# Moving the weighted sums, the low parts of the weights and the modulation stream in a one-core three-block forward pass

## Chip, cores and metric

One Trainium2 chip, one of its cores. The metric is the device time of one execution in microseconds; before the change it is 2541.97 us, the median of three runs (2541.0 to 2543.16).

## The reference, cut to what matters

Two blocks work on 512 tokens of width 2048. The first has an attention layer and a pooling layer, the second is a layer of stick-breaking attention and retention. Each layer computes `shift, scale, gate = silu(c) @ mod_w + mod_b`, normalises, multiplies with a large input matrix, mixes, gates with `silu(z)`, and multiplies with an output matrix. For this change the attention layer matters:

```python
s = jnp.einsum('bqkgd,bskd->bkgqs', q, k).astype(jnp.float32) * ATTN_SCALE
p = jax.nn.softmax(s, axis=-1).astype(v.dtype)
o = jnp.einsum('bkgqs,bskd->bqkgd', p, v)          # the weighted sum
y = jnp.concatenate([outA, outB], axis=-1) * jax.nn.silu(z)
```

There are 16 heads of 128. Heads 0 to 7 see all 512 tokens and 256 context rows; heads 8 to 15 see a band of up to 384 tokens, the 256 context rows and a sink. All of it is float32.

## The kernel before, in words

**Weights.** All weight matrices are one stream of 376 chunks of 128x1024 floats. SyncE loads chunk i into `RAW[i % 5]`. A float32 product is made from rounded parts: ScalarE copies the chunk to fp32r (`WHI[i % 4]`, the plan's stage "split"), VectorE subtracts (`WLO`, in the place of `RAW`, stage "low"), and TensorE adds hi*hi, hi*lo and lo*hi. ScalarE may round chunk i once TensorE has finished chunk i - 4; VectorE's subtraction waits for ScalarE's rounding of the same chunk.

**The plan.** `make_plan` writes one list of stages, and each engine's program walks the whole list and issues what it has for each stage. So the list fixes the order on every engine, and each engine is held up only by its semaphore waits. A matrix product of 128 tokens by 256 columns goes through `gemm`: 4 chunks, each of 4 steps ("mm" of 6 matmuls). After each step `step(background)` advances the background generators by one: this is how attention is put between matrix products. `split_ahead(i)` is called once per chunk, in its second step, ahead of that step's background work. It first puts "low" for every chunk that has a "split" but no "low", then "split" for chunk i + 3. So in the attention heads VectorE makes the low part of a chunk one chunk later in the list than ScalarE rounds it: where ScalarE rounds chunk i + 3, VectorE makes the low part of chunk i + 2.

**A pair of heads.** For p = 0 to 7 there are two products (q, then z), 32 steps, and `pair_task(p)` runs beside them and beside the next pair's q product. Its clock t counts steps from the first score row. There are eight score rows (two heads of four 128-query tiles, n = 0 to 7), put at t = 0, 3, 6, 9, 17, 20, 23, 26 (in the last pair the last four one step sooner). For a row TensorE makes the scores in PSUM (`ST`, two halves by turns), VectorE takes the maximum (L1925) and bounds it (L1684), ScalarE takes the exponential (L1498, or L1493 and L1495), and one step later in the list ("row_end") VectorE takes the reciprocal (L1947), scales (L1684) and transposes (L1952). After a head's last row SyncE writes the probabilities out ("turn", 4 steps later) and reads them back in another layout ("turn_in", 8 steps later). The weighted sum ("pv") of the head is put 20 (first head of the pair) or 19 steps after its last row, at t = 29 and t = 45, and "gate" (VectorE, Y<-ST,Y) one step behind it. A new pair starts every 32 steps, so t = 29 is 3 steps ahead of the next pair's row 0 and t = 45 is the next pair's t = 13. The weighted sum writes the PSUM bank `OB`, which is part of the half that rows with odd n use, so it waits for the exponential of the last odd row. The last head, 15, is moved by DMAs that SyncE and ScalarE issue (L1116) once the sum of head 14 has been made.

**Modulation.** `mod_stream` is a generator: each step loads 512 KB (SyncE, L1176) and adds 2 x 512 columns on VectorE (`MACC`, L1687). It is stepped once per chunk, and a second time in chunks whose number is in `at["extra"]`. In the heads it is stepped once per chunk.

**Layer changes.** `gemm_last`, then `gemm_three`: the last product of a layer, the norm, and the first products of the next layer. There too the low parts follow `split_ahead`.

Of the kernel before, what the change touches and what calls it, by code (L numbers as in the profile page):

```python
# [79 lines left out]
def build(nc, ctx, T, out):  # L80
# [26 lines left out]
    for i in range(NR):  # L107
        tile, at = place(f"RAW{i}", [P, 4, 256], F32)
# [4 lines left out]
    for i in range(2):  # L113
        tile, at = place(f"MRAW{i}", [P, 4, 256], F32)
# [233 lines left out]
    def make_plan():  # L348
# [1 line left out]
        todo = []  # L350
        background = []
        gates = [[], [], []]
        at = {"load": 0, "split": 0, "low": 0, "use": 0, "done": 0, "unit": 0, "pair": 0, "heads": False, "hold": False, "extra": ()}
        scored = []
        summed = set()
        pending = []
# [2 lines left out]
        def put(*stage):  # L359
            todo.append(stage)  # L360
# [14 lines left out]
            put("split", at["split"])  # L375
            at["split"] += 1

        def low_next():
            put("low", at["low"])
            at["low"] += 1  # L380

        def split_ahead(i):
            while at["low"] < at["split"]:
                low_next()
            while at["split"] < min(i + NS, len(chunks)):
                split_next()

        def low_until(i):
            while at["low"] <= i:
                low_next()  # L390

        def step(gens):
            for g in list(gens):
# [13 lines left out]
        def unit(work, quiet=False):  # L407
            u = at["unit"]
            at["unit"] += 1
            n = len(units[u])  # L410
            at["pair"] += n // 8 + 1
            for c in range(n):
                i = at["use"]
                at["use"] += 1
                while at["split"] <= i:
                    split_next()
                low_until(i)
                work(u, i, c, c == n - 1)
                used(i)
                if not at["heads"]:  # L420
                    reduce_pending()
                if not (quiet and c >= n - 2 or at["hold"]):
                    step([mods])
                    if c in at["extra"]:
                        step([mods])
            return u
# [15 lines left out]
        def gemm_three(layer, tiles):  # L442
            first = at["pair"] % 2
            for pair in range(3):
                gated(pair)
            pairs = (first, 1 - first, 2)
            u, i0 = at["unit"], at["use"]
            at["unit"] += 1
            at["pair"] += 2
            at["use"] += 12  # L450
            next(tiles)
            split_ahead(i0 - 1)
            low_until(at["split"] - 1)
            next(tiles)
            for jj in range(2):
                for uu in range(3):
                    low_until(i0 + uu)
                    for nt in range(2):
                        put("mm2", "h", layer, u, i0 + uu, uu, 0, nt, jj, pairs[uu])
                    if jj:  # L460
                        used(i0 + uu)
                    if (jj, uu) != (1, 0):
                        split_ahead(i0 + (uu if jj else 0))
                        low_until(at["split"] - 1)
                    if (jj, uu) in ((0, 1), (1, 1)):
                        next(tiles)
            for c in range(3, 12):
                i, uu = i0 + c, c % 3
                low_until(i)
                for jj in range(2):  # L470
                    for nt in range(2):
                        put("mm2", "h", layer, u, i, uu, c // 3 * 4, nt, jj, pairs[uu])
                    if jj == 0:
                        split_ahead(i)
                        low_until(at["split"] - 1)
                        next(tiles, None)
                used(i)
                if layer == 2 and c >= 8:
                    reduce_pending()
                    step([mods])  # L480
            return u, first

        def gemm_last(layer):
            pair = at["pair"] % 2
            gated(pair)
            u, i0 = at["unit"], at["use"]
            at["unit"] += 1
            at["pair"] += 1
            at["use"] += 4
            spare[layer] = 1 - pair, i0 + 4  # L490
            s = 0
            for nt in range(2):
                for c in range(4):
                    low_until(i0 + c)
                    for jj in range(2):
                        put("mm", "y", layer, u, i0 + c, c, nt, jj, pair, c == 3)
                        if jj == 0:
                            if nt == 0:
                                split_ahead(i0)
                            elif c in (1, 2):  # L500
                                split_ahead(i0 + c)
                        step(background)
                        if s == 7:
                            put("o_copy", layer, 14, pair, 0, u, (u, 0))
                        elif s == 8:
                            put("o_more", layer, 14)
                        elif s in (11, 13, 14):
                            put("o_sum", layer, (11, 13, 14).index(s))
                        s += 1
                    if nt:  # L510
                        used(i0 + c)
                    elif c % 2:
                        reduce_pending()
                        step([mods])
            return u, pair
# [93 lines left out]
        def prologue():  # L609
            for i in range(8):  # L610
                put("job_load", i)
            for n in range(6):
                for q in range(4):
                    put("x_turn", n, q)
                put("x_sum", n)
            put("x_rstd")
            ready, near = [], []
            for i, (nb, c) in enumerate(jobs0):
                n = i // 4
                put("job_row", i)  # L620
                if i + 8 < len(jobs0):
                    put("job_load", i + 8)
                if i in (1, 3, 5):
                    load_next()
                if c == 3:
                    put("row_copy", n)
                if i == 3:
                    put("x_cast")
                if i in (9, 11, 13):
                    split_next()  # L630
                    low_next()
                    loads()
                if c == 1 and n > 0:
                    put("row_cols", n - 1)
                    ready += near
                    near = []
                    if n % 2 == 0:
                        put("h_pair", n // 2 - 1)
                        near = pieces(n // 2 - 1)
                if i > 51 and i % 4 == 3:  # L640
                    put("x_spill", i // 4 - 13, i)
                for _ in range((0, 2, 0, 3)[i % 4]):
                    if ready:
                        kv_piece(*ready.pop(0))
            put("row_cols", len(order0) - 1)
            put("h_pair", 7)
            put("x_spill", 3, 63)
            for piece in ready + near + pieces(7):
                kv_piece(*piece)
            at["unit"], at["use"], at["pair"] = 1, 8, 2  # L650
# [8 lines left out]
        def kv_piece(k, what, part):  # L659
            put("kv", k, what, part)  # L660
            if k % 4 == 3 and part == (1 if what == "k" else 2):
                used(at["done"])
                split_next()
                low_next()

        prologue()

# [19 lines left out]
        for i in range(3):  # L687
            put("v_copy", 0, i, 1, 0)
        task = chain([norm_rope(("k", 0), True), norm_rope(("kc", 0), True),
                      norm_rope(("k", 1), True), norm_rope(("kc", 1), True)])  # L690
        background.append(task)
        u, pair = gemm("hc", 1)
        finish(task)
        for nt in range(2):
# [1 line left out]
        task = chain([norm_rope(("k", 2), False), norm_rope(("k", 3), False)])  # L696
        background.append(task)
        pair = at["pair"] % 2
        at["extra"] = (0, 1, 2, 3)
        u = gemm_tok(1, 6, pair)  # L700
        at["extra"] = ()
        for i in range(3):
# [18 lines left out]
        def pair_task(p):  # L721
# [15 lines left out]
            def later(t, *stage):  # L737
                events.setdefault(t, []).append(stage)
# [7 lines left out]
            t, last_y = 0, 12  # L746
            while events:
                for what, *a in reversed(events.pop(t, [])):
                    if what == "rows":
                        i, qt = divmod(a[0], 4)  # L750
                        h, n = 2 * p + i, 8 * p + a[0]
# [4 lines left out]
                        if qt == 3:  # L756
                            later(t + 4, "turn", h)
                            if h < 15:
                                later(t + 8, "turn_in", h)
                            later(t + (10 if h == 15 else 20 - i), "pv", h)  # L760
                    elif what == "pv":
                        put("pv", *a)
                        later(t + 1, "gate", *a)
# [23 lines left out]
        for p in range(8):  # L787
            u, pair = gemm("h", 1)
# [887 lines left out]
    def dve_program(e):  # L1676
# [48 lines left out]
        for stage, *a in plan:  # L1725
# [43 lines left out]
            elif stage == "h_pair":  # L1769
                i, = a  # L1770
# [20 lines left out]
                for k in (2 * i, 2 * i + 1):  # L1791
                    e.wait_ge(a_h, ("c", k))
                    stt(CLO[:, k, :], TM[:, k % 2 * CTX:k % 2 * CTX + CTX], MODX[:, k:k + 1], f(CHI[:, k, :]), ADD,
                        SUB).then_inc(*v_h.up(("c", k)))
            elif stage == "low":
                i, = a
                e.wait_ge(a_whi, i)
                tt(WLO[i % NR][:, :, :], RAW[i % NR][:, :, :], f(WHI[i % NS][:, :, :]), SUB).then_inc(*v_wlo.up(i))
# [903 lines left out]
```

## Time and profile before

| | us |
|---|---|
| median of three runs | 2541.97 |
| the profiled execution | 2541.1 |
| its span, first to last instruction | 2539.1 |
| TensorE busy | 2463.3 (97%) |
| VectorE busy | 1713.5 (67%) |
| ScalarE busy | 932.6 (37%) |

The profile is of one execution. Its own time is 2.0 us over its span and 0.9 us under the median. Times in a timeline count from the first instruction. The attention heads lie between 258.7 us (the first maximum) and 787.9 us (the last).

### The profile page before, as it was taken

The page shows a single profiled execution, that of the slowest core. Times are in us where ns is not written, and L with a number is a line of the kernel's source. Part 1 is how long each engine was busy: PE and PEld are TensorE (multiplying, and loading weights), DVE is VectorE, ACT ScalarE, POOL GpSimd, SP SyncE. Part 2 cuts the span into 40 slices and gives each one's busy share as a digit, 9 for nine tenths or more (in the row PEclk, how much of TensorE's full clock was granted, in tenths as well). Part 3 has the DMA queues.
Part 4 walks back from the last instruction along what each step waited for, and adds up shares of the span by engine and source line. Part 5 has one row for each costly group of instructions (what it writes and reads, how often), then busy time and mean ns, then how long its engine had stood idle before and what let it go on. Part 6 is the DMA issues. An engine that isn't in the chain of part 4 may idle for free.

```text
span 2539.1 us, 29369 instructions
## 1 busy us (share of the span) xinstructions
PE 2463.3 (97%) x11527; PEld 1983.2 (78%) x11527; DVE 1713.5 (67%) x2634; ACT 932.6 (37%) x1453; POOL 111.5 (4%) x117
## 2 busy tenths in 40 slices
PE   7999999999889999999999999999999999999999
PEld 4789777777667887888888887888888787887887
DVE  4456888888877778776877767456455577666622
ACT  4232333333334333432334433445355432333421
POOL 0000000000000114000000113000000000000000
PEclk8999999999999999999999999999999999999999
DMA  9955678777766764666655754422222245532342
GB/s 348 337 187 189 203 206 223 214 220 207 203 180 188 256 197 151 204 203 215 203 166 170 253 182 136 125 83 84 83 84 83 81 144 166 178 120 83 126 156 83
DMA packets 345660, 439.32 MB, mean 173 GB/s; under 512 B 13154, under 2 KB 271842, under 8 KB 339762
## 3 DMA queue, kind: packets, MB, share of 16 engines
q1 hardware_dynamic: 338048, 403.82, 51.5%
q0 software_dynamic: 5808, 32.84, 3.4%
q8 instruction: 91, 1.49, 0.2%
q10 hardware_dynamic: 1666, 0.79, 0.1%
q14 instruction: 47, 0.39, 0.1%
HBM read 395.44 MB, written 40.37 MB: 172 GB/s over the span
## 4 chain that ended last, share of the span: by engine, by line
PE 79%; DVE 13%; ACT 2%; DMA 2%; issue 2%; SPq 1%; ACTq 0%; POOL 0%; DVEq 0%; POOLq 0%
PE G L2227 67%; PE ST L2227 12%; DVE SM L1925 2%; DVE MACC L1687 2%; DVE WLO L1681 1%; DVE PB L1952 1%; DVE PB L1684 1%; ACT PB L1498 1%; DMA MORE<-in_ev_mod_w 1%; DMA MRAW<-in_ev_mod_w 1%; DVE Y L1681 1%; DVE TT L1681 1%; PE ST L2230 0%; DVE SM L1684 0%; SPq L1162 0%
## 5 line engine op out<-in xcount | busy, mean ns | idle before, releaser
L2227 PE MATMUL G<-HHI,WHI 128*128 128x512 f32 x2596 | 1044.4, 404 | 2.9 <-DVE HLO L1681 2.4
L2227 PE MATMUL G<-HLO,WHI 128*128 128x512 f32 x2560 | 998.8, 390 | 2.4 <-DVE HLO L1687 2.4
L2227 PE MATMUL G<-HHI,WLO 128*128 128x512 f32 x2560 | 999.0, 390 | 0.0
L1325 ACT ACTIVATE WHI<-RAW 128x1024 fp32r<-128x1024 f32 x376 | 396.5, 1055 | 608.5 <-PE G L2227 547.0
L2227 PEld LDWEIGHTS G<-HHI,WHI 128*128 128x128 f32 x2596 | 488.8, 188 | 110.8 <-issue 7.7
L2227 PEld LDWEIGHTS G<-HLO,WHI 128*128 128x128 f32 x2560 | 481.4, 188 | 108.7 <-issue 7.7
L2227 PEld LDWEIGHTS G<-HHI,WLO 128*128 128x128 f32 x2560 | 480.6, 188 | 103.4
L1681 DVE TENSOR_TENSOR WLO<-RAW,WHI 128x1024 fp32r<-128x1024 f32 x376 | 460.7, 1228 | 93.8 <-ACT WHI L1325 93.5
L1687 DVE SCALAR_TENSOR_TENSOR MACC<-MWIDE,SC,MACC 128x512 f32<-128x512 f32 x420 | 320.8, 764 | 98.6 <-DMA MWIDE<-in_w_ada 48.1
L2227 PE MATMUL G<-WHI,HHI 128*128 128x512 f32 (+1 forms) x384 | 143.2, 373 | 0.6 <-ACT K L1325 0.6
L2227 PE MATMUL G<-WLO,HHI 128*128 128x512 f32 (+1 forms) x384 | 136.4, 355 | 0.0
L2227 PE MATMUL G<-WHI,HLO 128*128 128x512 f32 (+1 forms) x384 | 136.1, 354 | 0.0
L2227 PE MATMUL ST<-PT,VV 128*128 128x512 f32 (+2 forms) x192 | 93.7, 647 | 37.2 <-ACT PB L1498 34.5
L2227 PEld LDWEIGHTS ST<-PT,VV 128*128 128x128 f32 x192 | 42.2, 227 | 85.4 <-issue 77.6
L1322 ACT ACTIVATE SQ<-SQ 128x512 f32<-128x512 f32 x144 | 90.5, 628 | 28.4 <-DVE SQ L1687 25.2
L2227 PEld LDWEIGHTS G<-WHI,HHI 128*128 128x128 f32 x384 | 72.6, 189 | 18.3 <-issue 7.0
L2227 PEld LDWEIGHTS G<-WHI,HLO 128*128 128x128 f32 x384 | 72.7, 189 | 12.2 <-issue 1.7
L1498 ACT ACTIVATE PB<-ST,SM,COL 128x768 f32<-128x768 f32 x32 | 31.8, 994 | 135.0 <-DVE SM L1684 132.6
L2227 PEld LDWEIGHTS G<-WLO,HHI 128*128 128x128 f32 x384 | 72.7, 189 | 10.3
L1684 DVE TENSOR_SCALAR TM<-ST 128x512 f32<-128x512 f32 (+1 forms) x28 | 18.8, 672 | 78.8 <-ACT TY L1322 78.8
L1952 DVE STREAM_TRANSPOSE PB<-PB 128x768 f32<-128x768 f32 (+1 forms) x64 | 59.4, 928 | 2.2
L1925 DVE TENSOR_REDUCE SM<-ST 128x1 f32<-128x768 f32 (+2 forms) x64 | 54.6, 853 | 6.0 <-PE ST L2227 5.0
(273 smaller groups left out, 2431.2 us busy)
## 6 DMA issues: line engine op xcount, KB each, us to landing
RAW<-in_w_in SPq DMA_DIRECT2D x128, 512.0 KB, 3.7
MWIDE<-in_od_mod_w SPq DMA_DIRECT2D x96, 512.0 KB, 4.7
MWIDE<-in_w_ada SPq DMA_DIRECT2D x96, 512.0 KB, 4.7
RAW<-in_ev_w_in SPq DMA_DIRECT2D x80, 512.0 KB, 6.7
RAW<-in_od_w_in SPq DMA_DIRECT2D x64, 512.0 KB, 3.9
p_spill<-PB SPq DMA_DIRECT2D x15, 1536.0 KB, 6.3
PT<-p_spill SPq DMA_DIRECT2D x60, 384.0 KB, 7.6
MWIDE<-in_ev_mod_w SPq DMA_DIRECT2D x32, 512.0 KB, 4.6
```

The source lines that it names most:

```text
L1322: return e.o.activation(o, i, fn, bias=bias, scale=scale)
L1325: return e.o.activation(o, i, ACT.Copy, scale=scale)
L1498: e.o.activation(p_rows(qt, kt0, 6), by_block(row_of(qt, lo, 768)), ACT.Exp, bias=nm, scale=1.0 if banded(h) else q_root_of(h, qt), accum_ ...
L1681: return e.o.tensor_tensor(o, a, b, op)
L1684: return e.o.tensor_scalar(o, a, s1, s2, op0, op1) if op1 else e.o.tensor_scalar(o, a, s1, None, op0)
L1687: return e.o.scalar_tensor_tensor(out=o, in0=a, scalar=s, in1=b, op0=op0, op1=op1)
L1925: e.o.tensor_reduce(nm, row_of(qt, lo, 768), AX_X, MAX, negate=True).then_inc(*v_sm.up((h, qt, "row")))
L1952: e.o.transpose(rows, rows).then_inc(*v_sm.up((h, qt, "turned")))
L2227: return e.o.matmul(o, l, r, start=start, stop=stop, skip_group_check=True)
```

## The change: what it does

Three parts. The stage "low" is gone: VectorE makes a chunk's low part at the place of "split", directly behind ScalarE's rounding of the same chunk. The weighted sums are put at t = 32 and t = 48 (23 and 22 steps behind the head's last row), and that of head 14 at t = 23. The second modulation step per chunk is made in the four chunks of the product that comes before the one where it was.

```diff
         def split_ahead(i):
-            while at["low"] < at["split"]:
-                low_next()
             while at["split"] < min(i + NS, len(chunks)):
                 split_next()
-
-        def low_until(i):
-            while at["low"] <= i:
-                low_next()
...
         background.append(task)
+        at["extra"] = (0, 1, 2, 3)
         u, pair = gemm("hc", 1)
         finish(task)
...
         pair = at["pair"] % 2
-        at["extra"] = (0, 1, 2, 3)
         u = gemm_tok(1, 6, pair)
         at["extra"] = ()
...
-                            later(t + (10 if h == 15 else 20 - i), "pv", h)
+                            later(t + (10 if h == 15 else 14 if h == 14 else 23 - i), "pv", h)
...
-            elif stage == "low":
+            elif stage == "split":
                 i, = a
                 e.wait_ge(a_whi, i)
                 tt(WLO[i % NR][:, :, :], RAW[i % NR][:, :, :], f(WHI[i % NS][:, :, :]), SUB).then_inc(*v_wlo.up(i))
```

Every other call of `low_next` and `low_until` is deleted with them.

## Rows read from the trace of the kernel before

**Rows 1.** TensorE's waits, 258.7 to 812 us: engine, operation, releaser, total us, times, longest.
```profile
PE ST L2227 <- ACT PB L1498: 35.9, 15, 4.5
```

**Rows 2.** TensorE's timeline, five weighted sums: start, us, engine, line, operation, [idle before].
```profile
482.79 5.39 PE L2227 MATMUL ST<-PT,VV 128*128 128x512 f32 x12 [0.66 <-ACT PB L1498]
...
548.28 8.37 PE L2227 MATMUL ST<-PT,VV 128*128 128x512 f32 x12 [3.23 <-ACT PB L1498]
...
652.50 5.80 PE L2227 MATMUL ST<-PT,VV 128*128 128x512 f32 x12 [2.90 <-ACT PB L1498]
...
791.58 4.03 PE L2227 MATMUL ST<-PT,VV 128*128 128x512 f32 x12
...
805.16 1.12 PE L2227 MATMUL ST<-PT,VV 128*128 128x512 f32 x2 [2.71 <-DMA PT<-PB]
```

**Rows 3.** Busy time by stretch: window, length, then engines, granted clock, DMA.
```profile
258.70:787.90 529.20, 491.85 (x2094) 378.26 (x2093) 439.10 (x767) 199.49 (x371) 0.00 (x0) 0.96 0.74 207
545.00:553.00 8.00, 4.77 (x7) 2.17 (x7) 6.62 (x14) 4.51 (x9) 0.00 (x0) 0.65 0.35 122
1617.00:2040.00 423.00, 422.42 (x1867) 342.70 (x1866) 230.81 (x377) 205.94 (x349) 0.00 (x0) 1.00 0.28 84
```

**Rows 4.** VectorE's waits for TensorE, 258.7 to 787.9 us, columns as in rows 1.
```profile
DVE COL L1684 <- PE ST L2227: 6.9, 3, 2.9
...
DVE ST L1681 <- PE ST L2227: 6.5, 8, 2.0
...
DVE SM L1925 <- PE ST L2227: 5.0, 5, 2.1
DVE Y L1681 <- PE ST L2227: 3.3, 2, 2.2
```

**Rows 5.** VectorE's timeline, the first and last low part behind a maximum.
```profile
266.65 1.22 DVE L1681 TENSOR_TENSOR WLO<-RAW,WHI 128x1024 fp32r<-128x1024 f32 x1
...
778.24 1.21 DVE L1681 TENSOR_TENSOR WLO<-RAW,WHI 128x1024 fp32r<-128x1024 f32 x1
779.85 0.22 DVE L1687 SCALAR_TENSOR_TENSOR SM<-SM 128x1 f32<-128x1 f32 x1 [0.39 <-ACT SM L1322]
```

**Rows 6.** ScalarE's timeline at the same places.
```profile
267.75 1.05 ACT L1325 ACTIVATE WHI<-RAW 128x1024 fp32r<-128x1024 f32 x1
...
779.72 1.05 ACT L1325 ACTIVATE WHI<-RAW 128x1024 fp32r<-128x1024 f32 x1
```

**Rows 7.** Behind a pair's last row: VectorE's low part, ScalarE's rounding; VectorE's statistics and reciprocal.
```profile
448.92 1.18 DVE L1681 TENSOR_TENSOR WLO<-RAW,WHI 128x1024 fp32r<-128x1024 f32 x1
...
448.92 1.08 ACT L1325 ACTIVATE WHI<-RAW 128x1024 fp32r<-128x1024 f32 x1
...
455.87 0.17 DVE L1684 TENSOR_SCALAR COL<-ST 128x8 f32<-128x8 f32 x1 [2.88 <-PE ST L2227]
455.95 0.69 DVE L1681 TENSOR_TENSOR Y<-ST,Y 128x512 f32<-128x512 f32 x1
...
463.49 0.16 DVE L1947 RECIPROCAL SM<-SM 128x1 f32<-128x1 f32 x1 [1.15 <-ACT PB L1498]
```

**Rows 8.** The end of the heads: VectorE's last maximum, then ScalarE's queue moving head 15.
```profile
787.89 0.69 DVE L1925 TENSOR_REDUCE SM<-ST 128x1 f32<-128x512 f32 x1
...
795.70 6.58 ACTq L1116 DMA_DIRECT2D PT<-PB  x8
```

**Rows 9.** A layer change: VectorE's two low parts; TensorE's waits from 812 us on.
```profile
966.29 2.35 DVE L1681 TENSOR_TENSOR WLO<-RAW,WHI 128x1024 fp32r<-128x1024 f32 x2
...
PE G L2227 <- DVE HLO L1687: 2.4, 4, 0.8
PE ST L2227 <- DVE WB L1681: 1.8, 1, 1.8
```

**Rows 10.** The product that gets the extra modulation steps: busy time (columns of rows 3), VectorE's timeline.
```profile
184.00:192.00 8.00, 8.00 (x51) 7.20 (x50) 7.61 (x14) 2.22 (x6) 0.00 (x0) 1.00 0.33 103
...
186.95 1.53 DVE L1687 SCALAR_TENSOR_TENSOR MACC<-MWIDE,SC,MACC 128x512 f32<-128x512 f32 x2
```

More of the change, by code:

```diff
@@ L352, in make_plan @@
         gates = [[], [], []]
-        at = {"load": 0, "split": 0, "low": 0, "use": 0, "done": 0, "unit": 0, "pair": 0, "heads": False, "hold": False, "extra": ()}
+        at = {"load": 0, "split": 0, "use": 0, "done": 0, "unit": 0, "pair": 0, "heads": False, "hold": False, "extra": ()}
         scored = []
@@ L376, in split_next @@
             at["split"] += 1
-        def low_next():
-            put("low", at["low"])
-            at["low"] += 1
         def split_ahead(i):
-            while at["low"] < at["split"]:
-                low_next()
             while at["split"] < min(i + NS, len(chunks)):
                 split_next()
-        def low_until(i):
-            while at["low"] <= i:
-                low_next()
         def step(gens):
@@ L416, in unit @@
                     split_next()
-                low_until(i)
                 work(u, i, c, c == n - 1)
@@ L452, in gemm_three @@
             split_ahead(i0 - 1)
-            low_until(at["split"] - 1)
             next(tiles)
@@ L456, in gemm_three @@
                 for uu in range(3):
-                    low_until(i0 + uu)
                     for nt in range(2):
@@ L463, in gemm_three @@
                         split_ahead(i0 + (uu if jj else 0))
-                        low_until(at["split"] - 1)
                     if (jj, uu) in ((0, 1), (1, 1)):
@@ L468, in gemm_three @@
                 i, uu = i0 + c, c % 3
-                low_until(i)
                 for jj in range(2):
@@ L474, in gemm_three @@
                         split_ahead(i)
-                        low_until(at["split"] - 1)
                         next(tiles, None)
@@ L493, in gemm_last @@
                 for c in range(4):
-                    low_until(i0 + c)
                     for jj in range(2):
@@ L630, in prologue @@
                     split_next()
-                    low_next()
                     loads()
@@ L663, in kv_piece @@
                 split_next()
-                low_next()
         prologue()
```

## The prediction

> **What bounds the kernel now.** I read TensorE's waits first. In the heads there is one that matters: 15 waits for the exponential, 35.9 us in all [rows 1], nearly all of them in front of a weighted sum. The second view is the timeline of those sums. One that waited 0.66 us took 5.39 us; one that waited 3.23 us took 8.37 us [rows 2], and the granted clock around it was 0.65 [rows 3]: a sum that starts behind a long wait runs partly at 1.2 GHz in place of 2.4. A banded one takes 5.80 us behind a wait and 4.03 without [rows 2]. Of the 16 sums, nine are stretched so: two dense by 1.7, one by 3.0, five banded by 1.8, one by 3.0, together 18 us. Read from TensorE alone, the heads hold 36 + 18 = 54 us to be had.
>
> The third view says otherwise. Over 529.2 us of heads, VectorE is busy for 439.1 [rows 3] and waits for TensorE for only 6.9 + 6.5 + 5.0 + 3.3 = 21.7 us [rows 4]. Its other idle time is waiting for ScalarE (a row's exponential between maximum and reciprocal) and gaps between instructions. So TensorE stands in front of the sums because VectorE is behind with its rows, and if TensorE never kept VectorE waiting the heads would still take 529.2 - 21.7 = 507.5 us. VectorE is the bound here, and what matters of an edit is what it does to VectorE's queue. Outside the heads TensorE is busy nearly all the time (422.4 of 423.0 us in stick-breaking, [rows 3]) and hardly waits [rows 9].
>
> **The change, part by part.**
>
> *Weighted sums three steps later.* Nothing is added or removed: 16 sums, 16 gates, the same DMAs. The stalls of at most about 4.5 us shrink by three steps, each of six matmuls at 0.227 us start to start, 4.1 us. What is won is bounded by what VectorE wins. The wait for the statistics of q, 2.9 us, comes from the sum that TensorE makes just ahead of them [rows 7]; with the sum behind them it goes. So do the waits for the first score row of each half, since the sum begins as soon as its exponential is there and fewer steps follow it. I take all 21.7 us as won, the most there is; the low end is none, if they come back elsewhere. The first head's gate, 0.65 us of VectorE, lands between a row's maximum and its reciprocal, where VectorE now idles 1.15 us [rows 7]: 7 times 0.65, 4.5 us won. Against that, the gate no longer covers ScalarE's rounding of q in the dense pairs: 0.7 us more in three pairs, 2.1. SyncE's queue: the read-back of the next head waits for the sum and now gets it three steps later, but its next load waits for a matrix product that TensorE ends later still, so nothing behind it moves; the read-back has 14 steps to its own sum. No cost.
>
> *Head 14's sum at t = 23.* The move of head 15 now waits for that sum and starts 795.7 - 787.9 = 7.8 us after the last maximum [rows 8]; without it it can start when the row is transposed, 3.7 us after it. 4.0 us won, as the sum of head 15 waits for this move [rows 2]. But 4.0 us of TensorE and one gate (0.7 us) move into the last rows, ahead of the last score row, and its own data were read back only some 10 us before. The nearest wait for such data is 2.71 us [rows 2]; between 0 and that I take 1.5 us, as VectorE's backlog covers part. Net 4.0 - 0.7 - 1.5 = 1.8 us won.
>
> *Low parts directly behind the rounding.* In the heads VectorE's list is unchanged but for an index: where it made the low part of chunk i + 2, whose rounding was long done, it makes that of chunk i + 3, and waits for the rounding at that place in ScalarE's list. Two such places in every pair stand between a row's maximum and its reciprocal. Now the low part starts at once and fills the time of the exponential: 266.65, next instruction 1.2 us later [rows 5]. But ScalarE rounds the next chunk only behind that exponential, 267.75 to 268.80 [rows 6]: VectorE would start at 268.80, 2.15 us later, with the exponential's time idle and the low part behind it. In the banded pairs it is 779.72 + 1.05 - 778.24 = 2.53 us, of which a wait of 0.39 behind it is saved [rows 5, 6]. I compared each low part from 257.6 to 786.5 us with the end of the next rounding. Sixteen places (first and last in [rows 5]) cost 2.15 to 2.53 us, 36.7 together. Three behind a dense pair's last row cost 448.92 + 1.08 - 448.92 = 1.08 each [rows 7], 3.2. Ten small ones cost 2.6. Sum 42.5 us, less four times 0.39: 40.9. The other places cost nothing, the rounding being done before VectorE arrives. All of it is idle time in the queue of the engine that bounds the stage. Low end: nothing, if VectorE had slack after all.
>
> The Trainium skill (PSUM — Partial Sum Buffer, section Engine vs sequencer instructions) calls the queues of ScalarE, VectorE and GpSimd strict FIFO. By that rule the reciprocal behind a waiting low part has no way past it, and the sum keeps the full 40.9.
>
> *Low parts at the layer changes.* Two low parts stand together between the norm's first tiles and the next ones, 2.35 us [rows 9]. One of them moves into idle time earlier: 1.1 us at each of two changes. TensorE's waits for those tiles are 2.4 us in all [rows 9]; I take 1.5 us won.
>
> *Low parts elsewhere.* In products without rows VectorE will often wait up to 6 us at a low part, but TensorE does not wait there now, and gets the low part a chunk sooner. In stick-breaking VectorE is busy 230.8 of 423.0 us [rows 3], which covers waits of up to 1.7 us per chunk. Zero; if that cover is thin, a few waits like the one of 1.8 us [rows 9].
>
> *Modulation four chunks sooner.* Four loads of 512 KB and four pairs of additions, 1.53 us each, 6.1 us of VectorE, move into a product where TensorE is busy 8.00 of 8.00 us and VectorE up to 7.61 [rows 10], out of one where VectorE waits for these loads. The low parts there are made at least 5 us ahead of use, and now a chunk sooner. SyncE's weight loads stand behind them in its queue, but DMA share is 0.33 [rows 10]. Zero; high end 6.
>
> **Sum.** Heads: -21.7 - 4.5 + 2.1 + 40.9 = +16.8; last heads -1.8; layer changes -1.5. Together +13.5 on the profiled execution of 2541.1: 2554.6. The median of before is 0.9 above it: **2555.5 us**, 0.5% slower.
>
> **Rivals.** *Faster: the low parts cost nothing, the sums win.* This is so if VectorE reaches the low parts no sooner than the rounding, or if the lag it builds up is drained in the gaps between rows. Then heads -21.7 - 4.5 + 2.1 = -24, and -3.3: 2515. It decides where VectorE's idle time between rows exceeds the 5 us per pair that the waits add. For it: 36 us of stalls are real. Against it: VectorE waits so little for TensorE [rows 4]. The far end is that TensorE alone is the bound and all 54 us go: 2488. The Trainium skill (TensorE: Matmul & The Clock Gate, section on HAM oscillation) says that a TensorE which keeps pausing between bursts falls back to its lower clock and pays again each time; by that rule alone the change wins the 18 us of stretched sums as well. That they are stretched the trace shows too [rows 2], but time that TensorE saves while VectorE is behind is only waited out later.
>
> *Half the cost.* The waits at the low parts overlap with waits that VectorE has anyway (for silu's exponential, for instance), so that 20 of 40.9 us count: 2555.5 - 20 = 2535, and with 30 of them 2545.
>
> *Worse: the sums win nothing.* The weighted sum now stands right ahead of a score row (t = 32, t = 48), so the row is delayed whenever the sum is. If VectorE's 21.7 us of waits come back there: 2555.5 + 21.7 = 2577. It decides if VectorE's lag at a pair's start is under 1 us.
>
> **How the numbers follow.** About 0.2% (5 us) can be told from no change here. The forecast has 0.52 (own range 2547 to 2563), faster 0.17, half the cost 0.19 (of it 0.08 below 2537 and 0.11 within 0.2%), worse 0.12. Faster by over 0.2%: 0.17 + 0.08 = 0.25; within: 0.11 + 0.02 from the forecast's lower edge = 0.13; slower: 0.50 + 0.12 = 0.62. The range 2526 to 2568 leaves out the faster case (less its upper edge) and the upper half of the worse one, together 0.2.
>
> **What the changed profile would show.** Right: VectorE's waits for `WHI` in the heads, near zero now, at 30 to 40 us, two of 2.1 to 2.5 us per pair, each directly behind a maximum; its waits for TensorE well under 10 us; sums at 5.39 and about 4.0 us in the clock's upper level in most pairs; head 15's move 4 us nearer the last maximum; everything from 812 us on shifted but not longer. The prediction is wrong if VectorE waits for the rounding less than 20 us in the heads, or if the heads, 258.7 to 787.9, get shorter.

## The result, and the profile after

The changed kernel takes **2573.89 us** (median; 2571.64 to 2575.46), the kernel before in the same comparison 2542.45: ratio 1.0128, 95% interval 1.0117 to 1.014. It is 31 to 33 us slower. The prediction had 2555.5 (2526 to 2568): the direction was right, but it forecast 13.5 us, less than half of what came, and the time lies outside the range. The profiled execution has a span of 2569.6 us against 2539.1.

First, where the time went. The first maximum stands at 257.70 and the last at 825.90 us, so the heads take 568.2 us in place of 529.2: 39.0 more. The move of head 15 gives 4.2 back (its sum starts at 838.94, 13.04 us behind the last maximum; 17.26 before). From that sum on there are 2569.6 - 838.94 = 1730.7 us, before 2539.1 - 805.16 = 1733.9: 3.2 less. With a first maximum 1.0 us earlier that is 39.0 - 4.2 - 3.2 - 1.0 = 30.6, the difference of the spans (30.5) to 0.1.

Busy time by stretch, the kernel after, columns as in [rows 3]: the heads; TensorE's stop at the end of the first pair and the stretch behind it.

```profile
257.70:825.90 568.20, 504.92 (x2099) 387.99 (x2098) 440.64 (x768) 198.65 (x371) 0.00 (x0) 0.94 0.69 192
312.00:317.00 5.00, 1.52 (x8) 1.55 (x8) 4.20 (x8) 3.81 (x7) 0.00 (x0) 0.82 0.22 57
317.00:325.00 8.00, 8.00 (x30) 6.61 (x31) 6.38 (x11) 2.23 (x5) 0.00 (x0) 0.69 0.77 293
```

VectorE is busy for 440.6 us in the heads, 1.5 more than before (439.1, [rows 3]). So nearly all that was lost is waiting, and its waits say for what. VectorE's waits in the heads, the kernel after (the rows that answer to [rows 4], and the new one):

```profile
DVE WLO L1662 <- ACT WHI L1306: 40.4, 28, 2.5
...
DVE SM L1906 <- PE ST L2208: 13.7, 3, 4.9
...
DVE ST L1662 <- PE ST L2208: 3.4, 2, 2.3
```

The wait for the rounding is 40.4 us. The waits for TensorE are 13.7 + 3.4 = 17.1, where [rows 4] had 21.7 and the prediction wanted none. VectorE's other waits for ScalarE are 54.6 us, 52.5 before. 40.4 - 4.6 + 2.1 + 1.5 (busy time) = 39.4 for the 39.0. The waits of up to 2.9 us for the statistics and those for the gates are gone; in their place stands one in front of a maximum, three times, up to 4.9 us each. What TensorE waits for changed likewise. Its waits from 257.7 to 845 us, the kernel after ([rows 1] is the answer of before):

```profile
PE ST L2208 <- ACT PB L1479: 19.6, 9, 3.6
PE ST L2208 <- ACT SQ L1303: 18.3, 3, 7.4
PE G L2208 <- DVE HLO L1662: 8.9, 4, 4.3
...
PE ST L2208 <- ACT PB L1476: 5.6, 3, 2.2
```

The 35.9 us of waits for the exponential are 19.6 + 5.6 = 25.2 us. Before, all but 1.4 of them stood in front of weighted sums; now only 15.8 do, the rest in front of score rows. And 18.3 us stand in front of the statistics of q (`ST<-ONE,SQ`), for ScalarE's square.

**The low part's wait, at the first place of [rows 5].** VectorE, then ScalarE, the kernel after:

```profile
264.23 0.21 DVE L1665 TENSOR_SCALAR SM<-SM,COL 128x1 f32<-128x1 f32 x1
266.54 1.23 DVE L1662 TENSOR_TENSOR WLO<-RAW,WHI 128x1024 fp32r<-128x1024 f32 x1 [2.10 <-ACT WHI L1306]
267.68 0.16 DVE L1928 RECIPROCAL SM<-SM 128x1 f32<-128x1 f32 x1
```

```profile
264.48 1.00 ACT L1479 ACTIVATE PB<-ST,SM,COL 128x768 f32<-128x768 f32 x1 [4.44 <-DVE SM L1665]
265.37 0.19 ACT L1479 ACTIVATION_READ_ACCUMULATOR PB<-ST,SM,COL 128x1 f32 x1
265.46 1.05 ACT L1306 ACTIVATE WHI<-RAW 128x1024 fp32r<-128x1024 f32 x1
```

The exponential and its sum are there at 265.56 and the reciprocal starts at 267.68: VectorE stands still for 2.10 us until the rounding ends (265.46 + 1.05 = 266.51), and the low part comes ahead of the reciprocal. The forecast for this place was 2.15. There are sixteen such places in the heads, of 2.10 to 2.48 us, 35.9 together (forecast: 36.7); the other twelve waits are shorter. The rule of the Trainium skill that the prediction used (PSUM — Partial Sum Buffer, section Engine vs sequencer instructions: these engines' queues are strict FIFO) agrees: nothing behind the low part passed it.

**A pair's end, where the sum was moved.** TensorE, the kernel before, then after:

```profile
311.14 7.08 PE L2227 MATMUL ST<-PT,VV 128*128 128x512 f32 x12 [4.27 <-ACT PB L1498]
318.06 0.95 PE L2227 MATMUL ST<-ONE,SQ 128*128 128x1 f32 x8
318.87 1.03 PE L2227 MATMUL ST<-ONE,TM 128*128 128x1 f32 x8
319.76 0.48 PE L2227 MATMUL G<-HHI,WHI 128*128 128x512 f32 x1
...
323.95 0.39 PE L2227 MATMUL ST<-KHI,QHI 128*128 128x512 f32 x1
```

```profile
315.48 1.84 PE L2208 MATMUL ST<-ONE,SQ 128*128 128x1 f32 x8 [4.75 <-ACT SQ L1303]
317.18 1.84 PE L2208 MATMUL ST<-ONE,TM 128*128 128x1 f32 x8
318.89 0.77 PE L2208 MATMUL G<-HHI,WHI 128*128 128x512 f32 x1
...
324.56 5.31 PE L2208 MATMUL ST<-PT,VV 128*128 128x512 f32 x12
329.31 0.79 PE L2208 MATMUL ST<-KHI,QHI 128*128 128x512 f32 x1
```

Before, TensorE waited 4.27 us for the last row's exponential, made the sum, the statistics, three steps and the next row. Now it waits 4.75 us at the statistics, then makes the same things in another order: statistics, three steps, sum, row. The stop is still there because the square stands behind that exponential in ScalarE's queue (the kernel after):

```profile
313.19 0.99 ACT L1479 ACTIVATE PB<-ST,SM,COL 128x768 f32<-128x768 f32 x1 [4.13 <-DVE SM L1665]
...
314.74 0.59 ACT L1303 ACTIVATE SQ<-G 128x512 f32<-128x512 f32 x1
```

In the kernel before, TensorE goes on 2.43 us after the pair's last maximum (308.71); in the kernel after it goes on 3.50 us after it (311.98): 1.07 lost. From there to the next row's first score it takes 12.81 us before and 13.83 after: 1.02 lost. What stands right behind the stop is slow, and that has changed places: the two groups of statistics take 3.41 us in place of 1.70 and the three steps 5.67 in place of 4.19, while the sum takes 4.75 in place of 6.92. The granted clock goes with it. The kernel before, to set beside the windows of the kernel after above:

```profile
313.00:317.00 4.00, 4.00 (x8) 1.76 (x7) 3.87 (x6) 1.07 (x2) 0.00 (x0) 0.71 0.97 390
317.00:325.00 8.00, 8.00 (x44) 6.48 (x43) 4.48 (x10) 2.00 (x4) 0.00 (x0) 1.00 0.39 130
```

It was 0.71 in the sum and 1.00 in the statistics and steps behind it; in the kernel after it is 0.69 in those from 317 to 325. The Trainium skill (TensorE: Matmul & The Clock Gate, section on HAM oscillation) warns of pausing between bursts; the trace agrees that a stop costs clock, but the stop was moved here and not removed.

VectorE, the kernel after: the last maximum, and what it does last before the next row; then the same row in the kernel before:

```profile
311.98 0.92 DVE L1906 TENSOR_REDUCE SM<-ST 128x1 f32<-128x768 f32 x1
...
325.14 1.22 DVE L1662 TENSOR_TENSOR WLO<-RAW,WHI 128x1024 fp32r<-128x1024 f32 x1
330.96 0.96 DVE L1906 TENSOR_REDUCE SM<-ST 128x1 f32<-128x768 f32 x1 [4.60 <-PE ST L2208]
```

```profile
325.19 0.96 DVE L1925 TENSOR_REDUCE SM<-ST 128x1 f32<-128x768 f32 x1 [0.29 <-PE ST L2227]
```

The wait for the statistics is gone (2.88 before) and 4.60 us for the row have come. From last to first maximum it is 330.96 - 311.98 = 19.0 us, 16.5 before. The 0.29 us of the kernel before matter: VectorE already waited for this row there, so it had no lag that could have covered a later one. It is so at the first row of every later pair: 0.29 us in the other two dense ones, 0.37 to 0.88 us (in front of the mask, `ST<-ST,MK`) in the banded ones.

### The profile page after: what moved, and what is told of

Same layout as the page of the kernel before. It is cut to its first block, busy times and chain, and to the rows that moved or that the text cites. A ratio compares the mean times of both kernels' runs of the same rounds, so it can differ in the third digit from the quotient of the medians.

```text
span 2569.6 us, 29369 instructions
## 1 busy us (share of the span) xinstructions
PE 2476.3 (96%) x11527; PEld 1994.2 (78%) x11527; DVE 1719.5 (67%) x2634; ACT 931.0 (36%) x1453; POOL 112.3 (4%) x117
## 4 chain that ended last, share of the span: by engine, by line
PE 73%; DVE 15%; ACT 4%; DMA 3%; issue 3%; SPq 1%; ACTq 0%; DVEq 0%
PE G L2208 63%; PE ST L2208 10%; DVE WLO L1662 2%; DVE MACC L1668 2%; DVE SM L1906 2%; DVE PB L1933 1%; DVE PB L1665 1%; ACT WHI L1306 1%; DVE TT L1662 1%; DMA p_spill<-PB 1%; DMA MRAW<-in_ev_mod_w 1%; ACT PB L1479 1%; DVE Y L1662 1%; DMA MORE<-in_ev_mod_w 1%; DVE QR L1662 1%
## 5 line engine op out<-in xcount | busy, mean ns | idle before, releaser
L1662 DVE TENSOR_TENSOR WLO<-RAW,WHI 128x1024 fp32r<-128x1024 f32 x376 | 458.7, 1221 | 369.1 <-ACT WHI L1306 367.3
L2208 PEld LDWEIGHTS G<-HHI,WHI 128*128 128x128 f32 x2596 | 492.8, 190 | 119.4 <-DVE HLO L1662 11.5
L2208 PE MATMUL ST<-PT,VV 128*128 128x512 f32 (+2 forms) x192 | 84.9, 598 | 16.9 <-ACT PB L1479 15.8
L1906 DVE TENSOR_REDUCE SM<-ST 128x1 f32<-128x768 f32 (+2 forms) x64 | 54.6, 852 | 14.8 <-PE ST L2208 13.7
L2208 PE MATMUL ST<-KHI,QHI 128*128 128x256 f32 (+2 forms) x128 | 42.9, 341 | 20.3 <-DVE QLO L1662 7.0
```

What stands on the lines that cost most here:

```text
L1662: return e.o.tensor_tensor(o, a, b, op)
L1906: e.o.tensor_reduce(nm, row_of(qt, lo, 768), AX_X, MAX, negate=True).then_inc(*v_sm.up((h, qt, "row")))
L2208: return e.o.matmul(o, l, r, start=start, stop=stop, skip_group_check=True)
```

## The experiments

Two theories. **A**: the low parts cost what was forecast (about 40 us), and the step that failed is the one that takes all 21.7 us of VectorE's waits for TensorE as won, above all where the sum moves behind the statistics. **B**: the low parts are cheap and the sums' new places are harmful in themselves. All kernels but two (the first and the change without three sums) start from the kernel before.

**Low parts alone.** The changed kernel with sums and modulation steps back:

```diff
-later(t + (10 if h == 15 else 14 if h == 14 else 23 - i), "pv", h)
+later(t + (10 if h == 15 else 20 - i), "pv", h)
```

> Low parts directly behind the rounding, weighted sums and modulation steps as before. Theory A (the low parts cost what was forecast for them, 40.9 us in the heads less 1.5 at the layer changes, and the whole change is slower than forecast because the sums won nothing): 2542 + 39 = 2581 if no wait of VectorE for TensorE hides behind them, down to 2567 if the 21.7 us of those waits absorb part; the row-maximum of the last row at least 25 us later than before. Theory B (the low parts are cheap, under 10 us, and the 31.4 us come from the sums' new places): 2535 to 2552.

Measured: 2582.73, ratio 1.0163 (1.0146 to 1.018), 41 us slower, with heads of 571.0 us, 41.8 longer than before. Theory B falls as an account of the 31 us; whether the sums' places harm as well is left to the runs below. VectorE's waits in its heads (263.5 to 834.5 us):

```profile
DVE WLO L1662 <- ACT WHI L1306: 40.0, 23, 2.5
...
DVE ST L1662 <- PE ST L2208: 7.7, 7, 2.3
DVE SM L1906 <- PE ST L2208: 7.1, 6, 2.7
DVE Y L1662 <- PE ST L2208: 5.1, 6, 1.4
DVE COL L1665 <- PE ST L2208: 4.7, 2, 2.9
```

Nothing is hidden: the waits for TensorE are 24.6 us, not less than 21.7.

**Sums alone.** The kernel before with the change's line for "pv" and nothing else:

> All weighted sums at their new places (t = 32, t = 48, head 14 at t = 23), low parts as before. Theory A (the sums' wait moves to the statistics of q and to the first row behind the sum, so they win nothing): within 6 us of 2542, with TensorE waiting about 18 us in front of the statistics for the square of q in the dense pairs. The prediction's own term (21.7 + 4.5 - 2.1 us won in the heads, 1.8 in the last ones): 2516. Theory B (the sums' places cost what the change costs): 2565 or more.

Measured: 2541.65, ratio 1.0004 (0.9994 to 1.0013). The sums alone win nothing: the measured change is 0 us (-1.5 to +3.3). TensorE's waits and VectorE's, this run, 257.7 to 850 us:

```profile
PE ST L2227 <- ACT SQ L1322: 11.5, 3, 5.3
PE ST L2227 <- DVE QLO L1681: 10.0, 3, 3.4
```

```profile
DVE SM L1925 <- PE ST L2227: 17.4, 5, 6.9
...
DVE ST L1681 <- PE ST L2227: 5.4, 2, 3.4
```

17.4 + 5.4 = 22.8 us of waits for TensorE, against 21.7: they have moved, not gone. In front of the statistics it is 11.5 us where 18 were expected. The 10.0 us stand in front of the first rows of banded pairs, 3.3 us at each of three, behind the moved sum: there are no statistics of q there, and the row waits for VectorE's `QLO`, not for the sum.

**Sums, but head 14's as before** (`20 if h == 14 else 23 - i`):

> As the run with all sums moved, but the sum of head 14 stays at t = 29. If its new place, ahead of the last score row and in the steps where the low parts of y are made, is what made the last pair 10 us longer in the changed kernel against some 3 in the others, this run is 4 to 6 us faster than the one with all sums moved. By the prediction's term (1.8 us won by moving it) it is 2 us slower.

Measured: 2543.97, ratio 1.0012 (1.0003 to 1.0022). Against the run before it head 14's place wins 2.3 us by the medians, where the prediction had 1.8, but the intervals overlap. The expectation that it made the last pair longer falls as an explanation of the total: from first to last maximum that pair is 60.2 us with it and 57.5 without (53.2 before), and the earlier move of head 15 gives more back. It also leaves 4.3 us of the last pair's growth. The likely cause is the sum of head 13, which now comes in the step of that pair's row 4; no run moved it alone.

**Modulation alone:**

```diff
+        at["extra"] = (0, 1, 2, 3)
         u, pair = gemm("hc", 1)
...
-        at["extra"] = (0, 1, 2, 3)
         u = gemm_tok(1, 6, pair)
```

> Only the second modulation step per chunk moved to the product ahead of the one where it was. Prediction's term zero: 2541 to 2543. High end: 6 us slower if VectorE's 6.1 us of additions come onto the path of the product that gets them.

Measured: 2539.48, ratio 0.9995 (0.9985 to 1.0004). No cost, as forecast.

**Which sums.** All at the new places but those of heads 0, 2 and 4 (`20 if h in (0, 2, 4) else 23 - i`), and the reverse, only those three:

> Low parts as before; all sums at their new places except those of heads 0, 2 and 4, whose new place (t = 32) comes behind the next pair's statistics of q. Theory A (there the wait only moves to the statistics; elsewhere the sums win what was forecast): in the run with all sums moved these three pairs began 3.3, 0.3 and 3.6 us later, start to start, than in the kernel before, so this run is 7 us faster than that one: 5 to 8 us faster than the kernel before (about 2535). Theory B (the sums win nothing at any place): as the kernel before, within 2 us.

> Low parts as before; only the sums of heads 0, 2 and 4 at t = 32. Theory A: 6 to 8 us slower than the kernel before (about 2549), TensorE waiting some 11 us for the square of q in front of the statistics, at the lower clock behind it. Theory B (the place costs nothing, other parts of the plan do): within 2 us of the kernel before. The prediction's term: some 9 us faster (2.9 us of the wait for the statistics and the stretched sums, in three pairs).

Measured: 2534.79, ratio 0.9969 (0.9957 to 0.9981), 8 us faster; and 2552.85, ratio 1.0044 (1.0028 to 1.0061), 11 us slower, somewhat more than the 6 to 8 expected. In the second TensorE waits 9.7 us for the square of q. VectorE's waits for TensorE, the first of the two, then the second, between their first and last maxima:

```profile
DVE ST L1681 <- PE ST L2227: 5.5, 2, 3.5
DVE COL L1684 <- PE ST L2227: 5.2, 3, 2.9
DVE SM L1925 <- PE ST L2227: 2.0, 5, 0.6
```

```profile
DVE SM L1925 <- PE ST L2227: 20.6, 5, 6.5
DVE ST L1681 <- PE ST L2227: 6.5, 8, 2.0
DVE Y L1681 <- PE ST L2227: 3.3, 2, 2.3
```

12.7 and 30.4 us, against 21.7: 9.0 less and 8.7 more. The heads are 523.6 and 537.7 us long, against 529.2: 5.6 less and 8.5 more. In the first, another 4.1 us are won behind the last maximum, most of it by the earlier move of head 15. So three of the sums lose what the others win.

**Where the low part stands.** In the attention heads each low part is put behind the background work of its step and not ahead of it, still a chunk sooner than before. Outside the heads it comes directly behind the rounding (that part of the edit is in the next run too):

```diff
                         if nt == 0 and jj:
                             split_ahead(i)
                         step(background)
+                        while at["low"] < at["split"]:
+                            low_next()
```

> Every low part directly behind its rounding except in the heads' products, where it follows the background work of the same step, so that a row's reciprocal, scaling and transposing come ahead of it; still a chunk sooner than before. Sums and modulation as before. Theory A (what costs is that the wait for the rounding stands between a row's maximum and its reciprocal): the 36.7 us of those places are gone, 2538 to 2547. Theory B (any wait for the rounding in the heads costs, since VectorE is the bound there): 2560 or more, VectorE's waits for the rounding still at 20 us or more. By Theory A those waits are under 12 us.

Measured: 2548.69, ratio 1.0027 (1.0016 to 1.0037): 7 us slower, of 41, and 1.7 us above the range of Theory A. The wait for the rounding fell from 40.0 to 3.5 us in the heads, as Theory A said (under 12); where it was 2.10 us, the reciprocal now follows the exponential directly, and the low part comes behind the row's last step:

```profile
266.30 0.16 DVE L1949 RECIPROCAL SM<-SM 128x1 f32<-128x1 f32 x1 [1.15 <-ACT PB L1500]
...
270.93 1.22 DVE L1683 TENSOR_TENSOR WLO<-RAW,WHI 128x1024 fp32r<-128x1024 f32 x1
```

The heads are 539.5 us here, 10.4 over the kernel before: 3.5 is the wait for the rounding that is left, and the waits for TensorE are 26.9 in place of 21.7 us, 5.2 more. The run shows that the cost goes when the waits go. It doesn't show what a wait as long would cost elsewhere in the heads, since hardly one is left.

**Low parts directly behind the rounding outside the heads only** (in `split_ahead`, behind the splits: `while not at["heads"] and at["low"] < at["split"]: low_next()`):

> Low parts directly behind the rounding in all stages but the attention heads; sums and modulation as before. Prediction's terms: 1.5 us won at the layer changes, zero elsewhere, so about 2540. In the changed kernel everything behind the heads took 3 us less than before: by that, 2538.5. If the waits of VectorE for the rounding outside the heads (274 us more in the changed kernel) counted at all, it is 2545 or more.

Measured: 2543.37, ratio 1.0006 (0.9996 to 1.0015). No difference in the whole. VectorE's waits for the rounding outside the heads are 320.9 us here, 93.5 in the kernel before, and that costs nothing that can be measured. (The 274 us in the expectation count the 40.4 us inside the heads too; outside them it is 326.9 - 93.5 = 233 in the changed kernel.) A win at the layer changes may be hidden here: `at["heads"]` ends before the last rows, so one low part in the last pair is still made between a row's maximum and its reciprocal, and waits:

```profile
783.61 1.23 DVE L1683 TENSOR_TENSOR WLO<-RAW,WHI 128x1024 fp32r<-128x1024 f32 x1 [2.47 <-ACT WHI L1327]
```

That pair is 3.3 us longer than in the kernel before. TensorE's wait for the norm's tiles, 2.4 us [rows 9], is 0.6 here. So the 1.5 us forecast for the layer changes are neither shown nor refuted.

**Sums one step and two steps later still** (`14 if h == 14 else 24`), behind a score row in place of right ahead of it:

> Low parts as before; all sums but those of heads 14 and 15 at t = 33 and t = 50, one and two steps later than in the change, so that each comes behind a score row and not right ahead of one. With all sums at the change's places (2541.65) VectorE waited 17.4 us in front of maxima for TensorE, nearly all of it at the first row behind heads 0, 2 and 4. Theory A (a sum costs by what it delays of VectorE's rows, and the wait for the square of q in front of the statistics stays, about 11 us of TensorE): the 17.4 us go, 5 to 8 of them are given back because the statistics still start late: 2528 to 2534. Theory B (what counts is TensorE's wait and the lower clock behind it, not the row): as with the change's places, 2540 to 2543.

Measured: 2547.74, ratio 1.0031 (1.0018 to 1.0043). Both theories missed. VectorE, this run, at the end of the first pair:

```profile
322.92 0.96 DVE L1925 TENSOR_REDUCE SM<-ST 128x1 f32<-128x768 f32 x1 [1.37 <-PE ST L2227]
...
333.27 0.96 DVE L1925 TENSOR_REDUCE SM<-ST 128x1 f32<-128x768 f32 x1 [0.38 <-PE ST L2227]
```

TensorE, this run, 257.7 to 820 us:

```profile
PE ST L2227 <- DVE Y L1681: 28.2, 7, 9.0
```

Against the run with all sums at the change's places, the first row came 5.3 us sooner behind the last maximum, as Theory A said, but the second only 1.8: the sum and a wait for it now lie between the two. At this place, the sum's own time falls in front of one row or the other. The 28.2 us are something else: all seven of those waits stand in front of a pair's sixth row, behind the second head's sum at t = 50. That row uses the bank that the sum wrote, and TensorE waits until VectorE has come to the gate that reads it.

VectorE's waits for TensorE are only 20.2 us here, less than before, yet the heads are 540.5 us long, 11.3 more. The rest is in its other waits for ScalarE, 63.3 us in place of 52.5, and 2.1 us of busy time: 10.8 + 2.1 - 1.5 = 11.4. The two that grew most:

```profile
DVE Y L1681 <- ACT SQ L1322: 17.0, 7, 3.1
...
DVE QLO L1681 <- ACT QHI L1325: 5.9, 7, 1.0
```

They were 12.7 and 1.3 us before. This run moved the second heads' sums too, so it doesn't test the first heads' place alone.

**The change without those three sums.** The changed kernel with heads 0, 2 and 4 at their old place:

> The whole change with the sums of heads 0, 2 and 4 back at t = 29. Theory A (their new place costs, with the low parts directly behind the rounding too): between the run with the low parts alone and the changed kernel the three gaps from a last row to the next first row grew by 1.3, 4.8 and 2.6 us, so 8.7 us less than the changed kernel: 2563 to 2567. Theory B (with VectorE behind by the low parts, a later sum wins everywhere): 2574 or more.

Measured: 2566.51, ratio 1.0105 (1.0089 to 1.012). By the ratios 6 us less than the changed kernel, by the medians 7: inside the range of Theory A. The heads are 562.0 us long, 6.2 less than in the changed kernel.

**The parts that win, together.** Sums without heads 0, 2, 4, and the modulation steps:

> All sums at the change's places except those of heads 0, 2 and 4, with the modulation steps four chunks sooner, low parts as before. The sums alone were 0.9969 of before, the modulation alone 0.9995 with an interval that holds 1: together 0.996 to 0.997, 2532 to 2535, below both kernels.

Measured: 2531.51, ratio 0.9963 (0.9951 to 0.9976), 9 us below the kernel before, half a microsecond below the expected range. It is faster than the kernel before and than the changed kernel; from the same sums without the modulation steps (0.9969) it can't be told apart.

## Why the prediction was wrong

**What held.** The heads can be added up from VectorE's queue. 507.5 us, the prediction's length of the heads without waits for TensorE, plus the waits for TensorE and for the rounding, gives 572.1, 530.3, 520.2, 537.9, 537.9, 558.4 and 565.0 for the runs with low parts alone, all sums, sums without three, those three alone, low parts behind the step, the change without three, and the change. Measured between the maxima: 571.0, 533.2, 523.6, 537.7, 539.5, 562.0 and 568.2. Two runs fit less well: the parts that win together (522.1, measured 527.6) and the sums behind a row (527.7, measured 540.5). What is missing is named by their profiles: with the changes of VectorE's other waits for ScalarE and of its busy time added, all of them come out within 1 us. Such a sum shows where the time went; that the low parts and the three sums caused it is shown by the runs that move them alone.

**Low parts: +40.9 forecast, 40.4 of wait in the change, 41 us measured alone.** The way it was found, each low part against the end of the next rounding, gave places and size right. The run that makes them behind the row's reciprocal has neither the waits nor most of the cost. Nothing was hidden: the rival with half the cost falls.

**The failed step: "I take all 21.7 us as won".** In the kernel before, the sums alone win 0 (interval -1.5 to +3.3), where the terms of the prediction give 24 and 1.8 for head 14. On top of the low parts they and the modulation steps win 9 (1.0163 to 1.0128). In the changed kernel 17.1 of the 21.7 us are left. Two sentences under it failed. "With the sum behind them it goes": the wait for the statistics did go, but TensorE's stop for ScalarE went to the statistics, which wait for a square that ScalarE makes behind the same exponential; the same work is left between the stop and the next row, and the order of it wins nothing. I had costed the moved sum by the wait that it left, and did not ask what the next instruction in TensorE's queue waits for. And "so do the waits for the first score row of each half": the sum now stood ahead of that row. At these three places the move costs 11 us by itself (1.0044); at the other 12 (head 14's among them) the waits for TensorE fell by 9.0 us, the heads by 5.6 and the time by 8.

This was the rival with the highest time, "the sums win nothing", at 2577; the result is 3 us below it, and its place, the row behind the sum, was right. It had 0.12 on the condition that VectorE has almost no lag at a pair's start. The trace of the kernel before could have settled that: VectorE waited for the first row of every pair but the first, 0.29 us in the three that matter. In the banded pairs the missing lag cost nothing: in three of the four the row waited for VectorE's own `QLO` and not for the sum, and in the other VectorE did not wait. The signs of being wrong that the prediction named (under 20 us of waits for the rounding, or shorter heads) did not come; the one that told was a sign of being right that failed, waits for TensorE "well under 10 us".

**The rest of the miss.** The heads were forecast 16.8 us longer and are 39.0 longer. Of the 22.2 us between, 17.1 are the failed step. Most of the rest are two small terms. The gate in idle time was to win 4.5; with all sums moved, VectorE's waits ahead of its row steps (`SM<-ACT PB` and the `SM<-ACT SM` of L1687) fell by 1.8 + 1.8 = 3.6. The wait for q's rounding was to cost 2.1; it grew from 1.3 to 5.9, and the waits for the square in L1687 from 1.3 to 4.1 without having been priced. In the changed kernel all of VectorE's other waits for ScalarE grew by 2.1, where the two terms make them shrink by 2.4.

**Other small terms.** Head 14: 1.8 forecast, 2.3 by the medians, with intervals that overlap. Layer changes: 1.5 forecast, not settled. Modulation: zero forecast, no difference measured.

**The last pair** took 63.1 us against 53.2, 9.9 more, where the others grew by 1.4 to 4.3. By the runs it is made up of the low parts (4.6 with these alone), the sums without head 14's (4.3) and head 14's (2.7 more), 11.6 together. TensorE's waits for `HLO`, 8.9 us in the changed kernel, lie in it. They come with the sums: 7.1 us with all sums but head 14's moved, 1.5 with the low parts alone.

## What to carry to other kernels

When an instruction is moved off a wait, look at what the next instruction of that engine waits for. If both wait for work behind the same instruction of another engine, the stop stays, and the moved work is now behind it and ahead of what follows. An instruction that comes up in its queue before its input is ready holds up everything behind it (2.1 to 2.5 us at each of sixteen places here); the lag of one chunk cost nothing in this kernel, and it filled the time of the other engine's round trip. Split a combined change by place: here three of fifteen moved sums gave back all that the others won.

## What the runs showed that was not expected

VectorE's waits for ScalarE's rounding grew from 93.5 us to 367.3 us over the whole kernel, 40.4 of it in the heads. Outside them a growth from 93.5 to 320.9 us cost nothing that can be measured, in the run that made only those low parts sooner (ratio 1.0006). The row of the kernel before, then the one of the page of after:

```profile
DVE WLO L1681 <- ACT WHI L1325: 93.5, 32, 6.3
```

```profile
L1662 DVE TENSOR_TENSOR WLO<-RAW,WHI 128x1024 fp32r<-128x1024 f32 x376 | 458.7, 1221 | 369.1 <-ACT WHI L1306 367.3
```

Waits of 227 us more lay outside the path; sixteen of 2 us each, between a row's maximum and its reciprocal, lay on it.
